# A decoder step on one core: the last gate tile copied raw, the gelus moved into the attention, the mixing behind them

## Chip, core and metric

The kernel runs on one core of one Trainium2 chip. The time is that of one execution on the device, in microseconds (us). Of several runs the median is given, and beside it the time of the one execution that was profiled.

## What is computed

One inference step of a hybrid decoder layer, for one new sequence of 512 tokens and eight sequences of four tokens each (544 tokens together), model width 1024, all in fp32. Cut to what matters here:

```
hn = _rmsnorm(x, g_pre_mix)
xl, gate, q, k, v, qi, ki, wi = _split_proj(hn @ w_in)
...
lru, hT, new_buf = _rglru(xl, conv_buf, h0, conv_w, conv_b, w_a, b_a, w_i, b_i, lam)
att = attend(q, k, v, qi, ki, wi)
mix = jnp.concatenate([lru * jax.nn.gelu(gate), att.reshape(B, T, ATTN_WIDTH)], axis=-1) @ w_out
x = x + _rmsnorm(mix, g_post_mix)
f = jnp.square(jax.nn.relu(_rmsnorm(x, g_pre_ffn) @ w_ff1)) @ w_ff2
x = x + _rmsnorm(f, g_post_ffn)
```

`_rglru` is a causal convolution of width 4, two sigmoid gates and a linear recurrence over the tokens, 512 channels. `attend` is sparse attention, 8 heads of width 64. For the 512 prompt tokens it goes over at most 512 keys, of which a mask keeps 128 for each token. For the 32 sample tokens it goes over 2048 cached keys and values in pages of 128, again under a mask. `lru * gelu(gate)` is the term whose pieces the change moves.

## The kernel before

The kernel is written by hand, engine by engine: each engine's program is a Python function that emits its instructions in a fixed order, and semaphores tie the engines together. Nothing is reordered by a scheduler. Everything is kept transposed, channels on the 128 partitions and the 544 tokens along the free dimension, in two halves of 272 (`HALF`).

**Products.** TensorE computes output tile after output tile into PSUM banks 0 to 3. Each half tile has a number; `gemm_mm` counts the finished ones, `gemm_ev` those that ScalarE has read out of PSUM. `E_GATE` is the first gate half, `E_WO` the first half of the output projection: when `gemm_ev` stands at `E_WO`, everything up to the last gate half is out of PSUM, and banks 0 to 3 are free for the attention.

**Gates.** The gate part has four tiles of 128 channels, in `mixT[:, 0:4, :]`. ScalarE copies the first three raw as they come (`gate_out`, L746 on). After the last step of the recurrence (`lru_root(3)`) it runs `gate_gelus`: gelu in place over tiles 0 to 2, then gelu straight from PSUM over the two halves of tile 3, which raises `gemm_ev` to `E_WO`. Square root, gelu and exponential each need a table load of their own on ScalarE.

**Attention over the prompt.** 32 units, `u = 8n + h`: query block n (0 to 3, with 128(n+1) keys) and head h. For each pair of units TensorE makes the scores (`att_scores`, banks 2 and 3), for each unit VectorE adds the mask and takes the maximum (`masked`), ScalarE the exponential with its sum (`exponentials`), VectorE divides (`normalized`), TensorE transposes (`att_transposes`, banks 6 and 7), ScalarE copies the transposes out (`transposed_out`), and for each pair TensorE multiplies with the values (`att_values`) and VectorE copies the result (`pair_out`). Each engine runs these steps in a loop over u, staggered: in turn u TensorE does the scores of u (even u), the transposes of u - 2 and the value pair u/2 - 2. The scores of a pair wait for both masks of the pair before (`pa_m`). Probabilities have four buffers, so `masked(u)` waits for the transposes of u - 4.

**Value products.** The sample attention's product with the cached values has 32 steps (`value_products(s)`, 4 matmuls in the program, 8 in the trace, about 1.0 us), into banks 4 and 5. Each needs four pages, 1 MB, in one of four slots. SyncE issues the transfers of step s as soon as product s - 4 has freed the slot (`values`, L399). Products 0 to 18 stand between the gate products, 19 to 31 in the attention: 19 in turn 0, then one in every third turn (20 in turn 1, 21 in turn 4, 22 in turn 7, 23 in turn 10, 24 in turn 13, and so on to 31 in turn 34). Slot 3 is in `regX`, the others are in `arena`.

**Others.** GpSimd waits for `gemm_ev` at `E_WO`, then loads the first half of the output weights (2 MB, L526). VectorE scales the first group of sample outputs (`sample_out(0)`) ahead of unit 0, and multiplies gate and recurrence (`mixed(c)`, L1172) in turns 8, 11, 14 and 17. The output projection waits for all units, all four mixings and the value pairs. Behind it come the MLP's products with split weights, about half of the run.

Of the kernel before, what the change touches and what calls it, by code (L numbers as in the profile page):

```python
# [16 lines left out]
ACT = mybir.ActivationFunctionType  # L17
# [8 lines left out]
HALF = NT // 2  # L26
# [5 lines left out]
CT = WIDTH // P  # L32
# [32 lines left out]
E_QI, E_KW, E_Q, E_K, E_V, E_XL, E_GATE, E_WO, E_MIX = 0, 8, 10, 18, 26, 31, 39, 47, 63  # L65
# [8 lines left out]
KSTEPS = GRP * NPG  # L74
# [2 lines left out]

V_ORDER = (4, 0, 1, 2, 3)
MID_VALUES = 19
NH_ORDER = (4, 5, 6, 7, 0, 1, 2, 3)  # L80
OUT_ORDER = ((0, 1, 2, 3, 4, 5, 6, 7), (4, 5, 6, 7, 0, 1, 2, 3))

# [7 lines left out]
def build(nc, xT_d, par_d, w_in_d, w_value_d, w_kw_d, w_out_d, w_mlp_d, wgate_d, ck_d, cv_d, ci_d, steps_d, pages_d,  # L90
          ident_d, rope_d, causal_d, ind_d, newmask_d, keyoff_d, yT_d, kT_d, v_d, kiT_d, lru_d):
    with ExitStack() as ctx:
# [87 lines left out]
        mixT = tiles(regM)  # L180
# [56 lines left out]
        half_cols = [slice(hf * HALF, (hf + 1) * HALF) for hf in range(2)]  # L237
# [305 lines left out]
        def _(eng):  # L543
# [7 lines left out]
            def gemm_out(e):  # L551
                eng.wait_ge(gemm_mm, e + 1)
                return bank[e % 4]
# [131 lines left out]
            def lru_root(c):  # L685
                eng.wait_ge(dd_rd, c + 1)
                nc.scalar.activation(dd, dd, ACT.Sqrt, scale=-1.0).then_inc(root_rd, 1)
# [60 lines left out]
                nc.scalar.copy(mixT[:, m, hf * HALF:(hf + 1) * HALF], src[:, 0:HALF]).then_inc(gemm_ev, 1)  # L748

            def gate_gelus():  # L750
                eng.wait_ge(gemm_ev, E_GATE + 6)
                for m in range(3):
                    nc.scalar.activation(mixT[:, m, :], mixT[:, m, :], ACT.Gelu_apprx_tanh).then_inc(gelu_rd, 1)
                for hf in range(2):
                    src = gemm_out(E_GATE + 6 + hf)
                    nc.scalar.activation(mixT[:, 3, half_cols[hf]], src[:, 0:HALF], ACT.Gelu_apprx_tanh).then_inc(gemm_ev, 1)

            sample_scores(30)
            sample_scores(31)
# [11 lines left out]
            def all_gates(c):  # L771
                for u in range(4):
                    lru_gates(c, u)
                lru_decay(c)
# [36 lines left out]
            lru_root(2)  # L811
            gate_out(2, 1)
            all_gates(3)
            lru_root(3)
            gate_gelus()

            def exponentials(u):
                nk = P * (u // NH + 1)
# [12 lines left out]
            for u in range(ATT_UNITS + 2):  # L831
                if u < ATT_UNITS:
                    exponentials(u)
                if u >= 2:
                    transposed_out(u - 2)
            load_tiles(eng, OUT1, range(CT))


# [105 lines left out]
        def _(eng):  # L944
# [221 lines left out]

            def mixed(c):

                eng.wait_ge(gelu_rd, min(c + 1, 3))
                eng.wait_ge(gemm_ev, E_WO)  # L1170
                eng.wait_ge(scan_rd, c + 1)
                vec.tensor_tensor(mixT[:, c, :], mixT[:, c, :], xl[:, c, 0:NT], ALU.mult).then_inc(mixed_rd, 1)  # L1172

# [57 lines left out]
            gated(3)  # L1231
            decayed(3)
            recurrent(3)
            sample_out(0)

            def masked(u):
                n, h = u // NH, u % NH
# [19 lines left out]
            for u in range(ATT_UNITS + 5):  # L1257
                if u < ATT_UNITS:
                    masked(u)
                if 1 <= u <= ATT_UNITS:  # L1260
                    normalized(u - 1)
                if u in (8, 11, 14, 17):
                    mixed((u - 8) // 3)
                if u >= 6 and u % 2 == 0:
                    pair_out((u - 6) // 2)

# [105 lines left out]
        def _(eng):  # L1372
# [388 lines left out]
            for u in range(ATT_UNITS + 5):  # L1761
                if u < ATT_UNITS and u % 2 == 0:
                    att_scores(u // 2)
                if 2 <= u < ATT_UNITS + 2:
                    att_transposes(u - 2)
                if 4 <= u < ATT_UNITS + 3 and u % 2 == 0:
                    att_values(u // 2 - 2)
                if u == 0:
                    value_products(MID_VALUES)
                elif u % 3 == 1 and MID_VALUES + 1 + u // 3 < KSTEPS:  # L1770
                    value_products(MID_VALUES + 1 + u // 3)

            def sample_out_transposes():
                for g in range(GRP):
# [185 lines left out]
```

## Time and profile before

| | us |
|---|---|
| median of 3 runs | 826.99 |
| lowest, highest | 825.69, 829.54 |
| the profiled execution | 830.0 |
| its span, first to last instruction | 828.2 |
| TensorE busy | 784.9 (95% of the span) |
| VectorE busy | 500.6 (60%) |
| ScalarE busy | 438.1 (53%) |
| mean granted TensorE clock | 0.983 of full |

The page divides the time by engine and by line; the chain that ended last says which work the end waited for. For a change of order, the timelines of single engines are the main view: each row has a start, a duration, and in square brackets the idle time ahead of it and what ended it. In the names, PE is TensorE, ACT ScalarE, DVE VectorE, POOL GpSimd, SPq the DMA issues of SyncE. `regX<-in_cv` is a transfer of cached values into slot 3.

### The profile page before, as it was taken

To read this page: it belongs to the slowest core of one execution; us is meant where nothing else is said; L and a number is where in the kernel's file an instruction comes from. 1 tells how busy PE (TensorE), PEld (TensorE's weight loads), DVE (VectorE), ACT (ScalarE), POOL (GpSimd) and SP (SyncE) were. 2 spreads that over 40 slices of the span, in tenths; PEclk is the share of its full clock that TensorE was granted. 3 is DMA by queue.
4 is the path that set the end of the run, shared out by engine and by line. 5 is a ranking of instruction groups with operands and counts; after the bars stand their busy time and mean duration, and the time that the engine had idled before them with its cause. 6 is when DMAs were issued, how large, how long until landed. Compare 5 with 4: busy or idle time off the path is not lost.

```text
span 828.2 us, 16951 instructions
## 1 busy us (share of the span) xinstructions
PE 784.9 (95%) x6187; PEld 655.8 (79%) x6187; DVE 500.6 (60%) x964; ACT 438.1 (53%) x881; POOL 101.5 (12%) x113
## 2 busy tenths in 40 slices
PE   5988999999999988999989999999999999999993
PEld 4862677745876643468879999999999999999993
DVE  4638999998664346621768786444446755544444
ACT  4546654412386574632457787534337777643440
POOL 0897453400000010000000000000000100000000
PEclk9998999999999998999999999999999999999997
DMA  8455339999649999460215555555555655555541
GB/s 325 138 169 159 122 134 370 384 393 362 223 134 353 326 340 355 147 248 17 76 55 175 178 175 169 173 172 175 177 177 178 214 173 176 177 178 176 170 161 54
DMA packets 69791, 166.89 MB, mean 202 GB/s; under 512 B 8995, under 2 KB 14628, under 8 KB 69348
## 3 DMA queue, kind: packets, MB, share of 16 engines
q1 hardware_dynamic: 64484, 145.54, 51.1%
q10 hardware_dynamic: 2592, 10.59, 3.6%
q0 software_dynamic: 2656, 9.98, 3.3%
q8 instruction: 36, 0.59, 0.3%
q14 instruction: 23, 0.19, 0.1%
HBM read 161.40 MB, written 4.67 MB: 201 GB/s over the span
## 4 chain that ended last, share of the span: by engine, by line
PE 78%; SPq 6%; ACT 5%; issue 4%; DVE 4%; DMA 2%; ACTq 0%; DVEq 0%
PE bank L1814 47%; PE bank L1393 14%; PE bank L1633 5%; SPq L399 5%; PE bank L1609 3%; PE bank L1731 1%; DMA regX<-in_cv 1%; PE bank L1503 1%; PE bank L1743 1%; SPq L394 1%; PE bank L1476 1%; DVE scp L1033 1%; PE bank L1756 1%; PE bank L1517 1%; DMA arena<-in_ck 1%
## 5 line engine op out<-in xcount | busy, mean ns | idle before, releaser
L1275 DVE TENSOR_TENSOR w_lo<-w_raw,w_hi 128x1024 fp32r<-128x1024 f32 x128 | 156.7, 1225 | 119.5 <-ACT w_hi L874 118.8
L874 ACT CAST w_hi<-w_raw 128x1024 fp32r<-128x1024 f32 x128 | 133.9, 1048 | 88.6 <-DMA w_raw<-in_w_mlp 88.6
L1814 PE MATMUL bank<-hn_hi,w_hi 128*128 128x272 f32 x512 | 148.6, 290 | 2.9 <-issue 2.9
L1814 PE MATMUL bank<-hn_hi,w_lo 128*128 128x272 f32 x512 | 148.8, 291 | 0.0
L1814 PE MATMUL bank<-h_lo,w_hi 128*128 128x272 f32 x512 | 148.4, 290 | 0.0
L1814 PE MATMUL bank<-hn_lo,w_hi 128*128 128x272 f32 x512 | 147.8, 289 | 0.0
L1814 PE MATMUL bank<-h_hi,w_hi 128*128 128x272 f32 x512 | 147.8, 289 | 0.0
L1814 PE MATMUL bank<-h_hi,w_lo 128*128 128x272 f32 x512 | 147.6, 288 | 0.0
L1814 PEld LDWEIGHTS bank<-hn_hi,w_hi 128*128 128x128 f32 x512 | 97.0, 190 | 3.4 <-issue 3.3
L1814 PEld LDWEIGHTS bank<-hn_lo,w_hi 128*128 128x128 f32 x512 | 97.1, 190 | 0.1
L1814 PEld LDWEIGHTS bank<-hn_hi,w_lo 128*128 128x128 f32 x512 | 96.9, 189 | 0.0
L1814 PEld LDWEIGHTS bank<-h_hi,w_hi 128*128 128x128 f32 x512 | 96.5, 188 | 0.0
L1814 PEld LDWEIGHTS bank<-h_hi,w_lo 128*128 128x128 f32 x512 | 96.4, 188 | 0.0
L1814 PEld LDWEIGHTS bank<-h_lo,w_hi 128*128 128x128 f32 x512 | 96.2, 188 | 0.0
L1393 PE MATMUL bank<-regM,wring 128*128 128x272 f32 x384 | 89.1, 393 | 0.0
L1393 PEld LDWEIGHTS bank<-regM,wring 128*128 128x128 f32 x384 | 72.8, 190 | 15.8 <-issue 0.8
L1393 PE MATMUL bank<-regR,wring 128*128 128x272 f32 x256 | 62.6, 398 | 0.0
L1393 PEld LDWEIGHTS bank<-regR,wring 128*128 128x128 f32 x256 | 47.5, 190 | 11.4 <-issue 2.4
L902 ACT ACTIVATE lx<-bank 128x272 f32<-128x272 f32 x64 | 25.5, 398 | 48.7 <-PE bank L1814 48.7
L1312 DVE TENSOR_TENSOR h_lo<-lx,h_hi 128x272 fp32r<-128x272 f32 x64 | 28.3, 442 | 34.6 <-ACT h_hi L908 33.7
L1287 DVE TENSOR_TENSOR regQ<-regQ 128x272 f32<-128x272 f32 x42 | 18.4, 440 | 47.6 <-ACT regM L916 19.2
L540 POOL DMA_DIRECT2D out<-regX x8 | 4.4, 544 | 289.0 <-DVE regX L1318 289.0
(260 smaller groups left out, 1209.8 us busy)
## 6 DMA issues: line engine op xcount, KB each, us to landing
w_raw<-in_w_mlp SPq DMA_DIRECT2D x128, 512.0 KB, 3.4
arena<-in_ck SPq DMA_DIRECT2D x96, 256.0 KB, 4.4
arena<-in_cv SPq DMA_DIRECT2D x96, 256.0 KB, 4.2
regQ<-in_ck SPq DMA_DIRECT2D x32, 256.0 KB, 4.5
regX<-in_cv SPq DMA_DIRECT2D x32, 256.0 KB, 3.9
wring<-in_w_in ACTq DMA_DIRECT2D x12, 512.0 KB, 5.9
wring<-in_w_in SPq DMA_DIRECT2D x8, 512.0 KB, 8.8
regX<-in_xT SPq DMA_DIRECT2D x4, 544.0 KB, 6.0
```

Source lines behind the costliest of these rows:

```text
L394: eng.load(page_regs, steps[0:1, bass.ds(s * 4, 4)])
L399: eng.dma_start(slot[:, b4, :], table[bass.ds(page[b4], 1), :, :].rearrange("a p c -> p (a c)")).then_inc(landed, 16)
L874: nc.scalar.copy(w_hi[n % 4][:, :], w_raw[n % 4][:, :]).then_inc(w_hi_rd, 1)
L902: nc.scalar.activation(relu_t[:, t % 2, :], bank[q % 4][:, 0:HALF], ACT.Relu).then_inc(mlp_ev, 1)
L1033: ins = vec.scalar_tensor_tensor(out=acc, in0=sm[:, u % 2, 0:nk], scalar=w, in1=acc, op0=ALU.mult, op1=ALU.add)
L1275: vec.tensor_tensor(w_lo[n % 4][:, :], w_raw[n % 4][:, :], w_hi[n % 4][:, :].bitcast(F32), ALU.subtract).then_inc(w_lo_rd, 1)
L1287: ins = vec.tensor_tensor(sqT[:, total, c], sqT[:, total, c], sqT[:, order[k], c], ALU.add)
L1312: vec.tensor_tensor(h_lo[:, at], square_t[:, t % 2, :], h_hi[:, at].bitcast(F32), ALU.subtract).then_inc(h_lo_rd, 1)
L1393: ins = pe.matmul(bank[e % 4][0:parts, 0:HALF], lhs(k), rhs[:, k, hf * HALF:(hf + 1) * HALF], start=(k == 0), stop=(k == KT - 1))
L1609: ins = pe.matmul(bank[4 + g][32 * b4:32 * b4 + 32, :], pT_rows[g][:, r, 32 * b4:32 * b4 + 32], v_slot[s % SLOTS][:, b4, :], start=(r == 0 ...
L1633: ins = pe.matmul(bank[e % 4][:, 0:HALF], lhs, rhs, start=(first and n == 0 and name == passes[0]), stop=(last and n == KT - 1 and name == ...
L1814: ins = pe.matmul(out, lhs[s][:, k * P:(k + 1) * P], rhs(k), start=(first and k == 0 and i == 0), stop=(last and k == KT - 1 and i == 2))
```

## The change

`gate_out` now copies tile 3 raw too, its first half ahead of `lru_root(3)`, its second behind it; the second copy raises `gemm_ev` to `E_WO`. `gate_gelus` becomes one group of four gelus over whole tiles, in ScalarE's turn 15 of the attention, behind `transposed_out(13)`. Value products 24, 25 and 26 go from turns 13, 16 and 19 to turn 17, all three in a row. `mixed` goes from turns 8, 11, 14, 17 to turns 21, 23, 25, 27, and `sample_out(0)` from ahead of unit 0 into turn 2. Line numbers grow by two or three.

```diff
+GELU_UNIT = 15
+VALUE_UNITS = (0, 1, 4, 7, 10, 17, 17, 17, 22, 25, 28, 31, 34)
...
             def gate_gelus():
-                eng.wait_ge(gemm_ev, E_GATE + 6)
-                for m in range(3):
+                eng.wait_ge(gemm_ev, E_WO)
+                for m in range(CT):
                     nc.scalar.activation(mixT[:, m, :], mixT[:, m, :], ACT.Gelu_apprx_tanh).then_inc(gelu_rd, 1)
-                for hf in range(2):
-                    src = gemm_out(E_GATE + 6 + hf)
-                    nc.scalar.activation(mixT[:, 3, half_cols[hf]], src[:, 0:HALF], ACT.Gelu_apprx_tanh).then_inc(gemm_ev, 1)
...
             all_gates(3)
+            gate_out(3, 0)
             lru_root(3)
-            gate_gelus()
+            gate_out(3, 1)
...
                 if u >= 2:
                     transposed_out(u - 2)
+                if u == GELU_UNIT:
+                    gate_gelus()
...
-                eng.wait_ge(gelu_rd, min(c + 1, 3))
-                eng.wait_ge(gemm_ev, E_WO)
+                eng.wait_ge(gelu_rd, c + 1)
...
             recurrent(3)
-            sample_out(0)
...
-                if u in (8, 11, 14, 17):
-                    mixed((u - 8) // 3)
+                if u == 2:
+                    sample_out(0)
+                if u in (21, 23, 25, 27):
+                    mixed((u - 21) // 2)
...
-                if u == 0:
-                    value_products(MID_VALUES)
-                elif u % 3 == 1 and MID_VALUES + 1 + u // 3 < KSTEPS:
-                    value_products(MID_VALUES + 1 + u // 3)
+                for i, at_unit in enumerate(VALUE_UNITS):
+                    if at_unit == u:
+                        value_products(MID_VALUES + i)
```

The order of instructions at the three places where it matters follows. First ScalarE from the end of the last recurrence step to the first exponentials, before (L753 and L756 are the gelus, L687 the root, L820 the exponentials):

```order
L683 ACTIVATE lx<-lx,sp 128x544
L687 ACT_TABLE_LOAD
L687 ACTIVATE lx<-lx 128x544 [waits dd_rd]
L753 ACT_TABLE_LOAD
L753 ACTIVATE regM<-regM 128x544 [waits gemm_ev]
L753 ACTIVATE regM<-regM 128x544 x2
L756 ACTIVATE regM<-bank1 128x272 [waits gemm_mm]
L756 ACTIVATE regM<-bank2 128x272 [waits gemm_mm]
L820 ACT_TABLE_LOAD
L820 ACTIVATE arena,stat<-arena,stat 128x128 [waits pa_m] x2
```

And the same place in the changed kernel (L750 is the raw copy, L689 the root):

```order
L750 COPY regM<-bank1 128x272 [waits gemm_mm]
L689 ACT_TABLE_LOAD
L689 ACTIVATE lx<-lx 128x544 [waits dd_rd]
L750 COPY regM<-bank2 128x272 [waits gemm_mm]
L820 ACT_TABLE_LOAD
L820 ACTIVATE arena,stat<-arena,stat 128x128 [waits pa_m] x2
```

One table load and five gelus have gone from ahead of the exponentials; two copies stand on either side of the root. The second place is ScalarE around the attention's turn 15 in the changed kernel (L755 the gelus, L820 exponentials of units 15, 16 and 17, L829 copies of units 13, 14 and 15; before, the rows of L755 and the second load are not there):

```order
L820 ACTIVATE regR,stat<-regR,stat 128x256 [waits pa_m]
L829 COPY arena<-bank7 128x256 [waits pa_t]
L755 ACT_TABLE_LOAD
L755 ACTIVATE regM<-regM 128x544 [waits gemm_ev]
L755 ACTIVATE regM<-regM 128x544 x3
L820 ACT_TABLE_LOAD
L820 ACTIVATE arena,stat<-arena,stat 128x384 [waits pa_m]
L829 COPY regR<-bank6 128x256 [waits pa_t]
L820 ACTIVATE arena,stat<-arena,stat 128x384 [waits pa_m]
L829 COPY regR<-bank7 128x256 [waits pa_t]
```

Two table loads now stand between two exponentials. The third place is TensorE from the scores of unit 16 to those of unit 18, before (L1731 scores, L1743 transposes, L1756 value pairs, L1609 value products):

```order
L1731 MATMUL bank<-arena,regQ 128x384 [waits pa_m]
...
L1743 MATMUL bank<-ident,regR 128x128 [waits pa_te,pa_n]
...
L1756 MATMUL bank<-arena 64x128 [waits pa_oe,pa_te]
...
L1609 MATMUL bank<-arena 32x512 [waits v_in1]
L1609 MATMUL bank<-arena 32x512 x3
L1743 MATMUL bank<-ident,regR 128x128 [waits pa_te,pa_n]
...
L1731 MATMUL bank<-arena,regQ 128x384 [waits pa_m]
```

And after (L1733 scores, L1745 transposes, L1758 value pairs, L1611 value products):

```order
L1733 MATMUL bank<-arena,regQ 128x384 [waits pa_m]
...
L1745 MATMUL bank<-ident,regR 128x128 [waits pa_te,pa_n]
...
L1758 MATMUL bank<-arena 64x128 [waits pa_oe,pa_te]
...
L1745 MATMUL bank<-ident,regR 128x128 [waits pa_te,pa_n]
...
L1611 MATMUL bank<-arena 32x512 [waits v_in0]
...
L1611 MATMUL bank<-arena 32x512 [waits v_in1]
...
L1611 MATMUL bank<-arena 32x512 [waits v_in2]
...
L1733 MATMUL bank<-arena,regQ 128x384 [waits pa_m]
```

Before, product 25 alone stands ahead of the transposes of unit 15; after, products 24, 25 and 26 stand behind them.

## Rows read from the trace of the kernel before

**Rows 1.** The page's chain that ended last: share of the span by engine.
```profile
PE 78%; SPq 6%; ACT 5%; issue 4%; DVE 4%; DMA 2%; ACTq 0%; DVEq 0%
```

**Rows 2.** Timeline of ScalarE at the handover: start, duration, instruction, idle before.
```profile
299.66 1.28 ACT L753 ACT_TABLE_LOAD   x1
300.95 1.75 ACT L753 ACTIVATE regM<-regM 128x544 f32<-128x544 f32 x3
302.61 0.66 ACT L756 ACTIVATE regM<-bank 128x272 f32<-128x272 f32 x2
303.29 1.28 ACT L820 ACT_TABLE_LOAD   x1
304.58 0.40 ACT L820 ACTIVATE arena<-arena,stat 128x128 f32<-128x128 f32 x1
```

**Rows 3.** Timeline of TensorE, units 0 to 20.
```profile
300.59 1.06 PE L1609 MATMUL bank<-arena 128*32 128x512 f32 x8
303.32 0.49 PE L1731 MATMUL bank<-arena,regQ 64*128 64x128 f32 x4 [1.67 <-ACT regM L756]
...
316.54 1.93 PE L1609 MATMUL bank<-regX,arena 128*32 128x512 f32 x8 [0.32 <-DMA regX<-in_cv]
...
319.02 1.23 PE L1731 MATMUL bank<-arena,regQ 64*128 64x256 f32 x4
...
322.47 1.24 PE L1609 MATMUL bank<-arena 128*32 128x512 f32 x8
323.64 0.70 PE L1731 MATMUL bank<-arena,regQ 64*128 64x256 f32 x4
...
326.50 0.92 PE L1731 MATMUL bank<-arena,regQ 64*128 64x384 f32 x4 [0.73 <-DVE stat L1243]
...
333.23 0.92 PE L1731 MATMUL bank<-arena,regQ 64*128 64x384 f32 x4
```

**Rows 4.** Timelines of VectorE and of GpSimd's DMA issues.
```profile
302.09 0.75 DVE L1193 TENSOR_SCALAR regR<-bank,sstat 128x512 f32<-128x512 f32 x1
...
313.44 0.72 DVE L1172 TENSOR_TENSOR regM<-regM,arena 128x544 f32<-128x544 f32 x1
...
336.95 0.56 DVE L1243 CUSTOM_DVE_ANT_0 regR<-bank,scp 128x384 f32<-128x384 f32 x1 [0.47 <-PE bank L1731]
...
303.56 2.10 POOL L526 DMA_DIRECT2D wring<-in_w_out  x4 [23.21 <-ACT regM L756]
```

**Rows 5.** The chain that ended last, in order of time, 300 to 330 us.
```profile
306.90 9.60 DMA regX<-in_cv
...
325.18 0.72 DVE regM L1172
```

**Rows 6.** Timeline of SyncE's DMA issues, value steps 21 to 23.
```profile
300.18 3.55 SPq L399 DMA_DIRECT2D arena<-in_cv  x6
305.03 2.29 SPq L399 DMA_DIRECT2D regX<-in_cv  x4
```

**Rows 7.** DMA issues of 304 to 308 us: count, KB each, median us to landing.
```profile
regX<-in_cv SPq DMA_DIRECT2D x4, 256.0 KB, 8.8
```

**Rows 8.** Busy time by stretch: us, five engines, granted clock, DMA share, GB/s.
```profile
302.00:304.00 2.00, 0.68 (x8) 0.46 (x12) 0.96 (x4) 1.98 (x5) 0.44 (x1) 1.00 0.98 313
...
314.00:316.00 2.00, 1.24 (x10) 0.70 (x10) 1.64 (x9) 0.79 (x4) 0.00 (x0) 1.00 1.04 395
316.00:318.00 2.00, 1.68 (x12) 0.20 (x8) 1.93 (x7) 1.42 (x5) 0.00 (x0) 0.51 1.06 388
...
322.00:324.00 2.00, 2.00 (x14) 0.64 (x14) 0.18 (x1) 0.72 (x3) 0.00 (x0) 0.78 1.06 388
```

**Rows 9.** Timeline of ScalarE around turns 15 to 17.
```profile
326.98 0.35 ACT L829 COPY arena<-bank 128x256 f32<-128x256 f32 x1
328.04 0.61 ACT L820 ACTIVATE arena<-arena,stat 128x384 f32<-128x384 f32 x1 [0.71 <-DVE stat L1243]
...
329.79 0.35 ACT L829 COPY regR<-bank 128x256 f32<-128x256 f32 x1
```

## The prediction

> **What bounds the kernel now.** I read the chain that ended last first. Four fifths of it are TensorE [rows 1], so the change moves the end of the kernel only by what it moves of the start of the output projection, which follows the 32 attention units without a gap. Nothing behind that is edited. So the question is what paces TensorE from 300 to 361 us.
>
> I then read ScalarE, TensorE and VectorE in order of time, from the last gate product on. **Stretch 1, the handover (300.6 to 303.3).** TensorE ends its last gate work and value product 18 at 301.65 and idles 1.67 us until ScalarE has released `E_WO` [rows 3]. ScalarE spends that time on a table load and five gelus, and loads the table for the exponentials behind them: the first exponential starts at 304.58 [rows 2]. **Stretch 2, units 0 to 10.** Units are short here, and the three engines wait for each other. It ends at 316.54 with a wait of 0.32 us for the DMA of value step 23, whose four transfers were issued from 305.03 on [rows 3, 6]. The chain has 9.60 us of that DMA in it [rows 5]. Transfers issued then take a median of 8.8 us [rows 7], since all DMA engines are full (share 0.98 to 1.06, [rows 8]) and carry the output weights as well. **Stretch 3, units 10 to 16.** TensorE's granted clock falls to its lower level (1.2 GHz) at about 316.0, after 2 us with 1.24 us of work, and is back at 2.4 GHz at about 322.9 (0.78 is the mean of that slice, [rows 8]). **Stretch 4, units 16 on.** TensorE is nearly full: the scores of unit 16 start at 326.50, those of unit 20 at 333.23 [rows 3], and they set the pace.
>
> **The change part by part.** Times below are on the profile's clock (before: span 828.2, execution 830.0).
>
> *Part A, raw copy instead of gelus before unit 0.* The copies of tile 3 go one on either side of `lru_root(3)`. The product's last matmul leaves TensorE at 300.6, so the second copy (0.39 as the two halves in [rows 2] take 0.38 each) ends at about 301.1, where `E_WO` fell at 303.3 before. TensorE is then at value product 18 until 301.65, so unit 0 starts with no wait: **-1.67 us**. The exponential table load follows the copy directly, 301.1 to 302.4, hidden behind VectorE's scan (to 302.0) and the first scores. No more than 1.67 can be won here.
>
> *Part B, `sample_out(0)` from before unit 0 to behind unit 2.* Its main instruction takes 0.75 us and ended at 302.84 [rows 4], before the first scores were even started (303.32, [rows 3]): free before. A reciprocal belongs to it, some 0.9 us in all from the end of the scan on. In unit 2 it stands ahead of `masked(3)`, and the scores of the next pair wait for that mask. The two engines wait for each other in turn there, so little of it is hidden: I take **+0.8** (0.4 to 0.9).
>
> *Part C, mixing 0 out of unit 8.* 0.72 us, 0.64 to the next instruction, ahead of `masked(9)`, for which TensorE waits [rows 4]: **-0.64**. So TensorE arrives at value product 23 at 316.22 - 1.67 + 0.8 - 0.64 = 314.7.
>
> *Part D, the DMA of step 23.* The same bytes have to land ahead of it. The output weights, issued by GpSimd at 303.56 on `E_WO` [rows 4], are now issued at 301.3. From 302 to 304 the DMA moved 313 GB/s, from 316 on 388 [rows 8]. Filling 2.3 us at the higher rate is 2.3 x 75 = 0.17 MB, at 388 GB/s 0.45 us earlier. Its own issue can come only 1.0 us earlier: SyncE is busy with the transfers of step 22 until 303.7 [rows 6], and the slot that it takes is free at 303.0. So it lands between 315.5 and 316.5; I take 316.0, as the queue was full, **-0.5**. The 1.5 us won above shrink to 0.5: TensorE waits 1.3 us instead of 0.32.
>
> *Part E, units 10 to 16 without value products 24 and 25.* Product 24 goes, 322.47 to 323.64: **-1.17**. The scores of unit 14 move up into the time at the low clock: 1.23 instead of 0.70 there, **+0.5**. Mixing 2 stood on the chain at 325.18 [rows 5] ahead of `masked(15)`: **-0.64**. Unit 16's scores start at 326.50 - 0.5 - 1.17 + 0.5 - 0.64 = 324.7. Mixing 1 fell into a VectorE wait, and counts for nothing.
>
> *Part F, the gelu group behind `transposed_out(13)`.* It is one load to gelu, four gelus, one load back: 1.28 + 4 x 0.553 (300.95 to 302.61 for three, [rows 2]) + 1.28 = 4.78 us. The copy of unit 13 ended at 327.33 [rows 9], now at 325.5; exponential 16 starts at 325.5 + 4.78 = 330.3 instead of 328.04. Queued behind the group on ScalarE are exponential 16, copy 14, exponential 17 and copy 15; VectorE's normalizations wait for the first, TensorE's transposes 16 and value pair 7 for the others. Meanwhile TensorE does the scores of unit 16, transposes 14, value pair 6, transposes 15 (to 326.9), then value products 24 to 26 (3 x 1.0, to 329.9), then the scores of unit 18 (to 330.8). Then it is out of work: transposes 16 wait for exponential and normalization (331.5), value pair 7 for copy 15. From exponential 16 to the end of copy 15 before were 2.1 us [rows 9], so copy 15 ends at 332.4; value pair 7 (0.6), transposes 17 (0.5) bring the scores of unit 20 to 333.5. Before they started at 333.23 [rows 3], product 26 included. So from unit 10 to 20 all that parts D and E won is given back: **+0.3 against before at unit 20**.
>
> The Trainium skill speaks against this part ("ScalarE: Activation LUTs", Table sets: the hidden batching unit): group calls by table set, and it counts a switch at about 2.7 us with the drain. The trace has 1.28 from the start of a load to the next instruction, twice [rows 2], with no drain. By the page's figure the group would be 2.8 us longer and the sum +3.3 at unit 20; the sum goes by the rows.
>
> *Part G, mixing in units 21, 23, 25, 27.* Each (0.72) stands just ahead of an even unit's mask, where VectorE waits for scores; the shortest such wait is 0.47 [rows 4], the others are longer. Cost 0.17 where it is short: **+0.2**. Without that cover it would be 4 x 0.64 = 2.6. Value loads 28 to 30 wait for the slots of products 24 to 26, free at 328 to 330; each is due at unit 25 or later (after 341): no wait.
>
> **Sum:** +0.3 + 0.2 = +0.5 on 830.0, so 830.5 for an execution like the profiled one. That execution is 3.0 above the median of the runs (826.99), so **827.5 us** on the scale of the runs. A measurement of this kernel can tell about 0.5%, 4.1 us, from no change.
>
> **The rivals.**
> *1. TensorE's clock doesn't fall at 316, or for less time (faster).* For: after 302 to 304, with 0.68 busy of 2 us, it did not fall, and that hole is now closed [rows 8]. Against: the wait ahead of product 23 gets longer, 1.3 us. 6.8 us at half clock cost up to 3.4 us; part E's +0.5 would go too, but VectorE and ScalarE then take part of it. I give it -3: 824.5.
> *2. A second fall after the gelu group (slower).* One mechanism: transposes 16 and value pair 7 wait for the four ScalarE steps behind the group. TensorE idles about 0.7 + 0.4 us from 330.8 to 332.4, about as much as just before the fall at 316 (0.76 of 2 us idle, [rows 8]). What follows is dense TensorE work, so 6.8 us at the low clock cost the full 3.4: 831. [...] Against: 3 us of unbroken value products stand ahead of it.
> *3. Output weights crowd step 22.* Issued 2.3 us earlier, they share the engines with load 22, issued 301.3 to 303.7. At step 23's latency (8.8, [rows 7]) it lands at 312. Product 22, which started at 310.97 and would be due 0.87 us earlier, waits 1.9 us, and product 23 comes at about 316.6 instead of 316.0: +0.6, 828.1. The Trainium skill ("DMA: Bandwidth & Descriptors", Queues, rings and completion order) has each DMA engine take turns between the queues that it has work for. By that rule, this rival holds; the 8.8 us beside the weights agree.
> *4. The landing follows the issue, and the group costs less.* Step 23 lands at 315.5 and TensorE meets copy 15 with no hole: -1.5, 825.5.
>
> **How the numbers follow.** My forecast with its small terms 0.50, rival 1 0.14, rival 2 0.16, rival 3 0.10, rival 4 0.10. All within 0.5%, except the far ends of rivals 1 and 2 together with the others' terms: faster by over 0.5% (under 822.9) 0.06, slower (over 831.1) 0.09, same 0.85. The range takes in rival 1 with a lighter end and rival 2: 823.8 to 831.2.
>
> **What would show it.** Right: no idle time before unit 0's scores; a wait of 1 to 2 us for `regX<-in_cv` before product 23; one gelu load and one exponential load 3.5 us apart at 325 to 330; a hole of about 1 us on TensorE behind the scores of unit 18; the output projection within 1 us of 361.3. Wrong: a second stretch at the low clock between 330 and 361, product 23 over 1 us earlier than 316.5, or a wait of the scores for VectorE in units 22 to 28.

## The result, and the profile after

The changed kernel takes 833.12 us (median of 16 executions, 830.97 to 836.13), the kernel before 828.13 beside it (16, 825.69 to 835.94). The ratio is 1.0057, interval 1.0040 to 1.0073: **slower by 4.7 us** by the ratio, by more than the 0.5% that the prediction set as its bound, and outside its range (823.8 to 831.2). The execution profiled took 834.25, its span 832.4, the mean granted clock 0.982.

Where the time went is best read on TensorE, measured from the start of value product 18 (the last one ahead of the attention) to the first matmul of the output projection, since the two profiled executions differ by 1.1 us already ahead of it. Timeline of TensorE of the changed kernel: start, duration, instruction, idle time before it and what ended that. They answer [rows 3] (L1611 are value products, L1733 scores, L1745 transposes, L1395 the output projection).

```profile
301.69 1.06 PE L1611 MATMUL bank<-arena 128*32 128x512 f32 x8
302.69 0.49 PE L1733 MATMUL bank<-arena,regQ 64*128 64x128 f32 x4
...
307.30 0.49 PE L1733 MATMUL bank<-arena,regQ 64*128 64x128 f32 x4 [0.74 <-DVE stat L1243]
...
314.76 1.93 PE L1611 MATMUL bank<-arena 128*32 128x512 f32 x8 [3.56 <-DMA arena<-in_cv]
...
321.70 1.94 PE L1611 MATMUL bank<-regX,arena 128*32 128x512 f32 x8
...
328.61 0.92 PE L1733 MATMUL bank<-arena,regQ 64*128 64x384 f32 x4
...
331.01 2.78 PE L1611 MATMUL bank<-arena 128*32 128x512 f32 x24
333.72 0.92 PE L1733 MATMUL bank<-arena,regQ 64*128 64x384 f32 x4
335.78 0.55 PE L1745 MATMUL bank<-ident,arena 128*128 128x128 f32 x3 [1.15 <-DVE arena L1250]
...
337.45 0.92 PE L1733 MATMUL bank<-arena,regQ 64*128 64x384 f32 x4
...
365.52 3.93 PE L1395 MATMUL bank<-regM,wring 128*128 128x272 f32 x16
```

The output projection of the kernel before, in the same view (the rows ahead of it are [rows 3]):

```profile
361.31 0.95 PE L1393 MATMUL bank<-regM,wring 128*128 128x272 f32 x3
```

| us after the start of value product 18 | before | after | difference |
|---|---|---|---|
| scores of unit 0 | 2.73 | 1.00 | -1.7 |
| value product 22, when TensorE is ready for it | 10.38 | 9.51 | -0.9 |
| value product 22 starts | 10.38 | 13.07 | +2.7 |
| value product 23 starts | 15.95 | 20.01 | +4.1 |
| scores of unit 16 | 25.91 | 26.92 | +1.0 |
| scores of unit 20 | 32.64 | 35.76 | +3.1 |
| output projection | 60.72 | 63.83 | +3.1 |

The handover works (no idle time before unit 0), then product 22 waits 3.56 us for its cached values. Before, it did not wait at all. The chain that ended last in the changed kernel has that transfer in it, and the weights' issue on GpSimd comes just ahead of it:

```profile
304.85 9.87 DMA arena<-in_cv
```
```profile
302.48 2.11 POOL L528 DMA_DIRECT2D wring<-in_w_out  x4 [21.02 <-ACT regM L750]
```

In [rows 4] the weights were issued at 303.56, that is 2.97 us behind the start of product 18; now it is 0.79 us. Step 22's four transfers were issued from 301.3 to 303.7 before, ahead of the weights; now from 302.9 to 304.85, beside and behind the four transfers of the weights. The DMA issues of the two stretches, count, KB each and median us to landing, first before (301.3 to 304), then after (302.9 to 304.9):

```profile
arena<-in_cv SPq DMA_DIRECT2D x4, 256.0 KB, 4.3
```
```profile
wring<-in_w_out POOLq DMA_DIRECT2D x4, 512.0 KB, 8.2
arena<-in_cv SPq DMA_DIRECT2D x4, 256.0 KB, 8.9
```

The latency doubled. And the clock, the second part of the loss, falls inside the wait. Busy time by stretch of the changed kernel (the five engines, granted clock, DMA share, GB/s), which answers [rows 8]:

```profile
310.00:312.00 2.00, 1.05 (x8) 0.48 (x6) 1.43 (x9) 1.29 (x6) 0.00 (x0) 1.00 1.03 410
312.00:314.00 2.00, 0.00 (x0) 0.00 (x0) 0.00 (x0) 0.00 (x0) 0.00 (x0) 0.96 1.03 398
314.00:316.00 2.00, 1.24 (x8) 0.20 (x8) 0.00 (x0) 0.00 (x0) 0.00 (x0) 0.50 1.05 394
...
322.00:324.00 2.00, 2.00 (x10) 0.29 (x2) 0.42 (x2) 0.60 (x2) 0.00 (x0) 0.50 1.08 384
324.00:326.00 2.00, 1.98 (x17) 1.07 (x16) 1.07 (x6) 1.01 (x4) 0.00 (x0) 0.98 0.80 248
```

TensorE has nothing to do from 311.2 to 314.76; at about 313.8 its clock falls to 1.2 GHz (0.96 is the mean of the slice to 314), and it comes back to 2.4 at about 324. So 9.3 us of work run at the low level, where it was 6.4 before (316.54 to about 322.9).

### The profile page after: what moved, and what is told of

Its sections match the earlier page's. It is cut to its first block, busy times and chain, and to the rows that moved or that the text cites. A ratio compares the mean times of both kernels' runs of the same rounds, so it can differ in the third digit from the quotient of the medians.

```text
span 832.4 us, 16953 instructions
## 1 busy us (share of the span) xinstructions
PE 786.7 (95%) x6187; PEld 656.7 (79%) x6187; DVE 499.9 (60%) x964; ACT 440.4 (53%) x883; POOL 100.8 (12%) x113
## 4 chain that ended last, share of the span: by engine, by line
PE 81%; ACT 4%; DVE 4%; DMA 4%; issue 4%; SPq 3%; ACTq 0%; DVEq 0%
PE bank L1815 47%; PE bank L1395 15%; PE bank L1635 5%; PE bank L1611 3%; SPq L401 2%; PE bank L1505 2%; PE bank L1733 1%; DMA regQ<-in_ck 1%; DMA arena<-in_cv 1%; DVE scp L1035 1%; PE bank L1519 1%; PE bank L1745 1%; PE bank L1478 1%; PE bank L1758 1%; DMA arena<-in_ck 1%
## 5 line engine op out<-in xcount | busy, mean ns | idle before, releaser
L1395 PE MATMUL bank<-regM,wring 128*128 128x272 f32 x384 | 89.6, 394 | 0.0
L1395 PEld LDWEIGHTS bank<-regM,wring 128*128 128x128 f32 x384 | 73.4, 191 | 16.0 <-issue 0.8
L1395 PE MATMUL bank<-regR,wring 128*128 128x272 f32 x256 | 62.6, 398 | 0.0
L1395 PEld LDWEIGHTS bank<-regR,wring 128*128 128x128 f32 x256 | 47.5, 190 | 11.4 <-issue 2.4
```

The costliest lines, as they stand in the source:

```text
L1395: ins = pe.matmul(bank[e % 4][0:parts, 0:HALF], lhs(k), rhs[:, k, hf * HALF:(hf + 1) * HALF], start=(k == 0), stop=(k == KT - 1))
```

## The experiments

**Theories.** *Weights:* the earlier release of `E_WO` lets GpSimd issue the 2 MB of output weights ahead of step 22's transfers; product 22 waits, the clock falls, and this is the whole loss. *Group:* the gelus and the displaced mixing and value products in units 15 to 20 cost more than parts A to E win. *Sample:* `sample_out(0)` in turn 2, with its wait of 0.74 us, is what starts it. Times of the kernel before are from the same chip in the same rounds.

All twelve, with the stretch from value product 18 to the output projection in the profiled execution, and the wait of TensorE for cached values:

| kernel | median, us | before beside it | ratio and interval | stretch, us | wait, us |
|---|---|---|---|---|---|
| before, weights late | 826.28 | 827.73 | 0.9988 (0.9976 to 1.0001) | 57.62 | 0 |
| after, weights late | 827.63 | 827.73 | 0.9991 (0.9974 to 1.0008) | 56.71 | 0 |
| before, weights early | 832.49 | 827.73 | 1.0056 (1.0034 to 1.0077) | 63.72 | 3.09 |
| after, values back | 836.43 | 827.73 | 1.0105 (1.0083 to 1.0127) | 65.61 | 3.08 |
| after, weights behind step 22 | 830.97 | 828.04 | 1.0036 (1.0018 to 1.0053) | 58.38 | 0 |
| after, weights late, values back | 830.54 | 828.04 | 1.0033 (1.0015 to 1.0051) | 59.82 | 0 |
| after, weights late, group at the end | 828.21 | 828.04 | 0.9997 (0.9982 to 1.0013) | 57.09 | 0 |
| after, weights late, sample first | 823.81 | 828.04 | 0.9957 (0.9940 to 0.9973) | 55.90 | 0 |
| after, sample first | 831.95 | 827.61 | 1.0057 (1.0035 to 1.0079) | 61.75 | 4.40 |
| before, sample in turn 2 | 828.58 | 827.61 | 1.0009 (0.9992 to 1.0025) | 61.44 | 0 |
| four products | 829.59 | 827.61 | 1.0014 (0.9997 to 1.0031) | 61.11 | 3.50 |
| four products, weights last | 823.54 | 828.02 | 0.9946 (0.9933 to 0.9959) | 55.19 | 0 |

### The weights, late and early

The first edit holds GpSimd's load of the output weights back until value product 23 is counted (`v_mm` 24), in the changed kernel and in the one before:

```diff
             eng.wait_ge(gemm_ev, E_WO)
+            eng.wait_ge(v_mm, 24)
             for m in range(CT):
                 eng.dma_start(wring[:, 0, m * PIECE:(m + 1) * PIECE], w_out_d[m]).then_inc(out_in[m], 16)
```

> The changed kernel, with one wait more on GpSimd: the output weights are issued only when value product 23 is done (24 steps), not on E_WO. Theory 1 (the weights, issued ahead of the transfers of value step 22, make product 22 wait 3.6 us and bring the low clock on early and for longer): the wait before product 22 goes, the low clock lasts at most 7 us, and the time falls by about 3 us against the changed kernel, to about that of the kernel before (ratio to before 0.998 to 1.002). Theory 2 (the gelu group with its two table loads inside the attention is what costs): the wait before product 22 may go, but the gain is under 1 us and the ratio stays at 1.004 or more.

> The kernel before, with the same wait on GpSimd: output weights issued behind value product 23. Theory 1: the DMA of step 23 lands 3 to 4 us earlier, TensorE no longer waits before product 23, the low clock from 316 on shrinks or goes, and the kernel is 1 to 3 us faster than before (ratio 0.996 to 0.999). Theory 2: no difference (ratio 1.000 within 0.001).

The second does to the kernel before what the change does to this load alone: it goes when the last gate half is computed and not when it is out of PSUM, with all else as it was.

```diff
-            eng.wait_ge(gemm_ev, E_WO)
+            eng.wait_ge(gemm_mm, E_WO)
```

> The kernel before, with the output weights issued when the last gate product has left TensorE (gemm_mm) instead of when ScalarE has read it (gemm_ev): about 2.5 us earlier, and nothing else changed. Theory 1: this alone costs 1 to 3 us (ratio 1.001 to 1.004), seen as a wait before value product 22 or 23 for its transfers. Theory 2: no cost, ratio 1.000 within 0.001.

Measured: with the weights late the changed kernel takes 827.63, and the loss is gone. The kernel before with late weights isn't clearly faster than as it was (0.9988, interval to 1.0001). With the weights early the kernel before takes 832.49, a ratio of 1.0056, as large as that of the whole change (1.0057) and more than the 1 to 3 us that were expected. Timelines of TensorE, then GpSimd, and the chain, of the kernel before with early weights:

```profile
316.18 1.93 PE L1609 MATMUL bank<-arena 128*32 128x512 f32 x8 [3.09 <-DMA arena<-in_cv]
```
```profile
303.01 2.10 POOL L526 DMA_DIRECT2D wring<-in_w_out  x4 [20.61 <-PE bank L1633]
```
```profile
306.22 9.92 DMA arena<-in_cv
```

It is the same wait at the same product for the same transfer, with no gelu, mixing or value product moved. Its clock falls twice for 3.4 us each (at about 315.7 and 322.6) where that of the changed kernel falls once for 10.2; the path to the projection is as long (63.72 and 63.83). Of the changed kernel with late weights, TensorE from product 18 over product 22 (310.04, no wait), units 16 and 20 to the output projection, GpSimd, and two of the stretches:

```profile
300.58 1.07 PE L1612 MATMUL bank<-arena 128*32 128x512 f32 x8
...
310.04 1.07 PE L1612 MATMUL bank<-arena 128*32 128x512 f32 x8
...
314.56 1.06 PE L1612 MATMUL bank<-regX,arena 128*32 128x512 f32 x8
...
320.37 0.92 PE L1734 MATMUL bank<-arena,regQ 64*128 64x384 f32 x4
...
329.21 0.92 PE L1734 MATMUL bank<-arena,regQ 64*128 64x384 f32 x4
...
357.29 3.93 PE L1396 MATMUL bank<-regM,wring 128*128 128x272 f32 x16
```
```profile
316.26 2.10 POOL L529 DMA_DIRECT2D wring<-in_w_out  x4 [35.91 <-PE bank L1612]
```
```profile
312.00:314.00 2.00, 1.50 (x11) 0.74 (x11) 1.60 (x10) 1.50 (x6) 0.00 (x0) 1.00 1.02 278
314.00:316.00 2.00, 2.00 (x18) 0.65 (x17) 1.75 (x9) 1.46 (x5) 0.00 (x0) 1.00 1.04 394
```

The four transfers of its step 22, with no weights issued yet (DMA issues of 301.7 to 304.5):

```profile
arena<-in_cv SPq DMA_DIRECT2D x4, 256.0 KB, 3.9
```

Product 23 has no wait either, the clock stays at its upper level through the attention, and the stretch is 56.71 us. What follows: the *weights* theory is right, and it is the whole loss.

The pair of late kernels also tells what the other parts of the change are worth with this disturbance out of the way. The kernel before with late weights, from product 18 over unit 16 to the projection:

```profile
299.33 1.06 PE L1610 MATMUL bank<-arena 128*32 128x512 f32 x8
...
322.15 0.92 PE L1732 MATMUL bank<-arena,regQ 64*128 64x384 f32 x4 [0.74 <-DVE stat L1244]
...
356.95 3.93 PE L1394 MATMUL bank<-regM,wring 128*128 128x272 f32 x16
```

The stretch is 56.71 against 57.62, **0.9 us less** on the path. The medians don't show it (827.63 and 826.28). The profiled execution of the changed one (824.47) is the fastest of its twelve. By the executions' mean clocks the rest may be the clock: all 12 of the kernel before with late weights have 0.987 or more, of the changed one 7 of 12 have 0.986 or less. What its clock fell at in those is in no profile.

### The value products back in their turns

```diff
-VALUE_UNITS = (0, 1, 4, 7, 10, 17, 17, 17, 22, 25, 28, 31, 34)
+VALUE_UNITS = (0, 1, 4, 7, 10, 13, 16, 19, 22, 25, 28, 31, 34)
```

> The changed kernel with value products 24, 25 and 26 back in turns 13, 16 and 19; the gelu group stays in turn 15 without cover. Theory 1: the wait before product 22 stays as it is; the group's hole on TensorE grows from 1.2 to about 3 us, of which part is won back where the products stood, so 1 to 2 us slower than the changed kernel (ratio to before 1.007 to 1.009). Theory 2 (the group is the cost): 3 us slower than the changed kernel (ratio 1.009 or more).

> Output weights late (behind product 23), gelu group in turn 15, value products 24 to 26 back in turns 13, 16 and 19. It shows the group's own cost where the DMA is out of the way. My theory: the hole behind unit 18's scores grows from 1.1 to about 3 us, and the three products cover the rest of it where they are moved: 1.5 to 2.5 us slower than with the three products in turn 17 (ratio to before 1.001 to 1.003), or up to 4 us slower if the clock falls behind the hole. Rival (placing products beside the group is worth nothing): same as with them in turn 17, ratio 0.998 to 1.000.

Measured: 3.3 us more than the changed kernel with the weights early (836.43 against 833.12, not on the same chip; ratios 1.0105 and 1.0057), and 2.9 us more with them late (830.54 against 827.63, again on two chips, ratios 1.0033 and 0.9991). The first of these, taken alone, is what was expected if the *group* theory held (1.009 or more). But the second kernel has the same group uncovered and no loss from the weights, and it stands at 1.0033: most of the 1.0105 isn't the group's. Behind the scores of unit 18, TensorE of the second (weights late) and the two stretches of 4 us around it, the timeline row first:

```profile
330.47 0.55 PE L1746 MATMUL bank<-ident,arena 128*128 128x128 f32 x3 [3.09 <-DVE arena L1251]
```
```profile
328.00:332.00 4.00, 1.53 (x14) 1.04 (x14) 2.13 (x8) 3.95 (x10) 0.00 (x0) 1.00 1.05 399
332.00:336.00 4.00, 4.00 (x18) 1.22 (x19) 1.21 (x7) 1.09 (x4) 0.00 (x0) 0.57 0.76 266
```

The hole is 3.09 us, where the three value products left 1.15, and the clock falls behind it (0.57 is a mean over four microseconds). So the moved products do what they are there for: they cover about 2 us of the group, and behind them the clock stayed up. The fall that rival 2 describes is here, behind a hole of 3.1 us; behind the hole of 1.15 there was none in the profiled execution of the changed kernel.

### The group behind the attention

```diff
-GELU_UNIT = 15
-VALUE_UNITS = (0, 1, 4, 7, 10, 17, 17, 17, 22, 25, 28, 31, 34)
+GELU_UNIT = ATT_UNITS + 1
+VALUE_UNITS = (0, 1, 4, 7, 10, 13, 16, 19, 22, 25, 28, 31, 34)
...
-                if u in (21, 23, 25, 27):
-                    mixed((u - 21) // 2)
...
+            for c in range(CT):
+                mixed(c)
```

> Output weights late, the gelu group and the four mixings behind the last attention unit, value products in their old turns. My theory: no hole in the middle and no table load back to the exponentials; instead the output projection waits 2 to 3 us for the group and the mixings at its end. Sum against the weights-late kernel between -1 and +1.5 us: ratio to before 0.998 to 1.001. Rival (the group costs its full 4.8 us wherever it stands): ratio 1.003 or more.

Measured: 828.21, no difference from before. In the attention nothing is lost, but the output projection waits for the gelus and mixings, and the clock falls there, at about 358.7. Its first row (the view names no engine for the wait; the four mixings, L1174, run from 356.12 to 358.75):

```profile
358.86 5.51 PE L1397 MATMUL bank<-regM,wring 128*128 128x272 f32 x16 [1.60 <-issue]
```

Its stretches there, with the same columns as the ones above:

```profile
356.00:360.00 4.00, 2.40 (x15) 1.09 (x12) 3.46 (x6) 1.73 (x4) 1.83 (x3) 0.84 0.88 306
360.00:364.00 4.00, 4.00 (x15) 3.12 (x14) 0.00 (x0) 0.00 (x0) 0.00 (x0) 0.74 1.09 450
```

The 16 matmuls take 5.51 us against 3.93 in the others. So a group at unit 15 is no worse than one that ends the attention (0.9991 and 0.9997). The place of the group isn't the loss, and that speaks against the *group* theory.

### Weights behind step 22 only

```diff
             eng.wait_ge(gemm_ev, E_WO)
+            eng.wait_ge(v_mm, 20)
```

> The changed kernel with the output weights held back until value product 19 is done (20 steps), at about 304 us: only 1.5 us later than in the changed kernel, but behind the last transfers of value step 22. Theory 1a (what counts is the place in the queues: whatever is issued behind the weights is late): product 22 waits for less than 1 us, product 23 takes the delay as in the kernel before, ratio to before 0.999 to 1.002. Theory 1b (2 MB more in the same stretch cost the same wherever they come in before product 23): product 22 or 23 waits 3 us or more, ratio 1.004 or more.

Measured: 830.97, spread 825.85 to 833.41, between the changed kernel and that with late weights. Of the two expectations neither is met: product 22 has no wait, as the first says, but the ratio is 1.0036. The profiled execution was the fastest one, a stretch of 58.38 with a short fall of the clock at product 21, so it doesn't show where the others lose their time. Its chain and its DMA issues (302.5 to 305) do show which step now stands beside the weights, issued at 301.88:

```profile
304.72 9.64 DMA regX<-in_cv
```
```profile
regX<-in_cv SPq DMA_DIRECT2D x4, 256.0 KB, 8.9
```

Step 23's data lands at 314.36 and its product starts at 314.41. TensorE comes no earlier only because of the fall at product 21: with the clock up it would be ready 13.98 us behind product 18, as in the kernel with late weights, at 312.7. My estimate from these rows is thus a wait of 1.6 us in such an execution. That the others lose their time there is not shown; that the threshold has to lie further back is.

### `sample_out(0)` first again, and in turn 2 of the kernel before

```diff
             recurrent(3)
+            sample_out(0)
...
-                if u == 2:
-                    sample_out(0)
```

> Output weights late, everything else as in the changed kernel, but the first sample output scaled ahead of unit 0 again. My theory: the wait of unit 4's scores for VectorE (0.74 us) goes, and the kernel gains 0 to 0.8 us against the one with the weights late (ratio to before 0.997 to 0.999), less if the exponential table load hides nothing of it. Rival: it delays the first mask by 0.9 us and the gain of the early handover is lost (ratio 1.000).

> The changed kernel with one edit undone: the first sample output is scaled ahead of unit 0 again; the output weights stay early. Theory 1 (the early weights are the cause, the move of the sample output costs its 0.8 us and little more): product 22 still waits 3 us or more, and the kernel is at most 1 us faster than the changed one (ratio to before 1.004 to 1.006). Theory 3 (the sample output in turn 2 is worth about 3 us wherever it stands, since it tips the clock): ratio 1.001 to 1.003.

> The kernel before with only the first sample output moved into turn 2. Theory 1: +0.8 us in the attention, of which the wait for the transfers of step 23 takes some back, ratio 1.000 to 1.001. Theory 3: more executions show the clock's fall, ratio 1.002 to 1.004.

Measured: the stretch gets 0.81 us shorter with the weights late (55.90 against 56.71), which is part B by its forecast of 0.8, and the kernel takes 823.81, **faster than before by 3.6 us** by the ratio. The median moved by 3.8 us between the two (2.8 by the ratios, as they ran on different chips), not by 0.8: its clocks are 0.989 or more in five executions of six, and those of the kernel that it is compared with only in two of twelve. With the weights early, sample first doesn't help: 831.95, ratio 1.0057 again, since product 22 is then due still earlier, and waits longer for its data:

```profile
313.13 1.94 PE L1610 MATMUL bank<-arena 128*32 128x512 f32 x8 [4.40 <-DMA arena<-in_cv]
```

Put into turn 2 of the kernel before, it makes no difference that the measurement can tell (828.58, 1.0009). A mean clock of 0.985 or less is in 5 of its 12 executions and in 5 of 23 beside it, too few to tell. The *sample* theory falls as the cause; it is a price of 0.8 us beside it.

### A fourth product under the group, and the best kernel

```diff
-VALUE_UNITS = (0, 1, 4, 7, 10, 17, 17, 17, 22, 25, 28, 31, 34)
+VALUE_UNITS = (0, 1, 4, 7, 10, 17, 17, 17, 17, 25, 28, 31, 34)
```

with sample first and weights behind product 23; the second kernel has this, and the weights behind product 28 (`v_mm` 29).

> Output weights late, first sample output ahead of unit 0, and value product 27 moved from turn 22 to turn 17 as well, so that four products stand beside the gelu group. The hole of 1.1 us behind unit 18's scores should be filled and about 1.0 us be won where product 27 stood: 1 us faster than with three products (823.8), ratio to before 0.993 to 0.996. Rival: the scores of unit 18 come 1.0 us later and the masks behind them hold up unit 20, so nothing is won (ratio as with three, 0.9957).

> As the kernel with four products beside the gelu group, but the output weights held back until value product 28 is done (29 steps, about 337 us), so that they stand behind the transfers of step 27 instead of beside them. Theory 1 (whatever value step is in transfer beside the weights comes 4 to 5 us late, and it costs when its product is due then): the 3.5 us wait before product 27 goes, no value product waits for a transfer, no fall of the clock in the attention, 823 us or less, ratio to before 0.993 to 0.996. Rival (four products in a row hold up the masks, and that is what cost): ratio 0.999 or more.

Measured: the first takes 829.59 (1.0014), worse than with three products (823.81), which neither expectation had. The weights, issued at 314.79, now stand ahead of step 27's transfers, and product 27 is due early:

```profile
327.58 1.94 PE L1611 MATMUL bank<-regX,arena 128*32 128x512 f32 x8 [3.50 <-DMA regX<-in_cv]
```
```profile
317.17 10.37 DMA regX<-in_cv
```

It is the loss of the changed kernel again, at another step, and the rival (the scores of unit 18 hold up the rest) isn't it, as the next kernel shows. With the weights last, the same product has its data, the hole under the group is down to 0.28 us, and the kernel is the best of all at **823.54, 0.9946 of before** (interval 0.9933 to 0.9959):

```profile
323.90 1.04 PE L1611 MATMUL bank<-regX,arena 128*32 128x512 f32 x8
...
326.07 0.55 PE L1745 MATMUL bank<-ident,arena 128*128 128x128 f32 x3 [0.28 <-DVE arena L1252]
...
355.12 3.93 PE L1395 MATMUL bank<-regM,wring 128*128 128x272 f32 x16
```

Its weights go at 337.97, 17 us ahead of the projection, and the projection has no wait. Against the kernel with three products (823.81, in another round) it can't be told apart.

## Why the prediction was wrong

*Parts A and B were right.* Unit 0's scores wait for nothing (1.67 forecast and won). Unit 4 waits 0.74 for the mask, and TensorE is ready for product 22 0.87 us earlier: -1.67 + 0.8. The runs with sample first put part B at 0.81.

*Part C was right where the data was there, and part E only by its sum.* Between the two kernels with late weights, from product 18, product 23 comes 1.56 us earlier (13.98 against 15.54). Product 22 is 0.92 earlier there (9.46 against 10.38), which leaves 0.64, part C's forecast. Unit 16 comes 3.0 us earlier (19.79 against 22.82): 1.47 for part E, forecast 1.31. But the 1.31 holds +0.5 for work at the low clock, and neither of these two kernels has a low clock there: without it the forecast would be 1.81, so that part of the agreement is luck.

*Part F was right.* From the scores of unit 16 to those of unit 20 the changed kernel takes 8.84 us where it was 6.73: +2.1; forecast 8.8. The group, from its load to exponential 16, on ScalarE of the changed kernel, which answers [rows 9]:

```profile
329.46 1.28 ACT L755 ACT_TABLE_LOAD   x1
330.76 2.30 ACT L755 ACTIVATE regM<-regM 128x544 f32<-128x544 f32 x4
333.07 1.28 ACT L820 ACT_TABLE_LOAD   x1
334.37 0.61 ACT L820 ACTIVATE arena<-arena,stat 128x384 f32<-128x384 f32 x1
```

4.91 us against 4.78. The sum went by the rows and not by the larger price of a table switch that the prediction quoted from the Trainium skill ("ScalarE: Activation LUTs", Table sets: the hidden batching unit), and the trace bears the rows out: 1.30 from the start of a load to the next instruction, both times. The hole behind unit 18's scores is 1.15 (forecast about 1.1 in two pieces). *Part G* was near: the difference stays at 3.1 from unit 20 to the projection, where +0.2 was forecast.

*Part D failed, and the loss on the path is in it.* It put product 23 at 316.0, 0.5 us earlier than before; it came at 320.6 on the clock of before (321.70 less the 1.1), 4.1 later. It asked whether the data of step 23 lands in time, and took for granted that step 22, whose wait was zero before, kept its data. Rival 3 asked that question and had the right mechanism; it mis-sized it. By it product 22 waits 1.9 us (landing at 312), product 23 comes at 316.6, the price is +0.6. Measured: a wait of 3.56, product 23 at 320.6 on the same clock. Two terms were wrong:
- *The landing.* I took step 23's 8.8 us from about 303.2, so 312. The last of step 22's transfers was issued at 304.85 and took 9.87: 314.7, or 313.6 on the clock of before. So it lands 1.6 later, 0.5 for the later issue (303.7 and not 303.2, and the last of the four is what counts) and 1.1 for the latency. The weights themselves went when part D said: 302.48 is 301.4 on the clock of before, forecast 301.3.
- *The clock.* Rival 3 costed the wait as shifted by idle time only, and let the fall stand at 316, as in [rows 8]. But the fall came ahead of the end of the longer wait (at about 313.8, 312.7 on the clock of before), and 9.3 us of work run at the low level instead of 6.4.

From -0.9 at product 22 these make +2.7 at its start and +4.1 at product 23. From there to unit 16 the changed kernel gives back 3.1, more than part E's 1.3, since only 2.3 us of its low clock are left behind the start of product 23, of 6.4 before; part F takes 2.1: +3.1.

*The size of the miss has two halves.* Forecast 827.5, measured 833.1. On the path +3.1 came for +0.5; that alone would have made 830.1, still inside the range. The other 3.0 us are the credit for the median, to which the next paragraph comes. That the halves add up to the measured 5.6 is in part chance: the two profiled executions differ by 1.1 us ahead of product 18 as well. Two slips of the prediction's sums change nothing in this: rival 4's -1.5 makes 826.0 and not 825.5, and with a group longer by 2.8 us, +3.3 is the whole sum and not the state at unit 20 (+3.1). Of its signs of being wrong none came (no low clock after 330, no product 23 over 1 us early, no long wait in units 22 to 28): none of them watched product 22. Of its signs of being right the wait before product 23 and the projection within 1 us of 361.3 (364.4 on the clock of before) failed.

*The profile I argued from was not the usual one.* Of the 86 executions of the kernel before that ran beside the experiments, 63 have a mean clock of 0.987 or more (median 827.45), 22 one of 0.985 or less (median 829.92). The one profiled, 830.0 at 0.983, is among the latter, while all 16 of the changed kernel have 0.979 to 0.983. What their clocks suggest, without a profile of one that shows it: in the usual execution of before, the clock doesn't fall ahead of product 23, just as it doesn't in the kernel before with late weights (57.62 us where the profiled one took 60.72). Against that, the loss is larger than the two profiles show, up to 63.83 - 57.62 = 6.2 us on the stretch; the ratio says 4.7 of the whole. To take 3.0 us off "for the median" was therefore to give the changed kernel a credit for high clocks that none of its 16 executions has. (Of the 16 executions of before the median is 828.13, so even for that kernel the credit would have been 1.9.) Rival 1 could have been read as a warning: it asked whether the fall of 316 is fixed, but only for the changed kernel.

*Rivals 1, 2 and 4 did not occur.* The low clock lasted longer, not shorter. Behind the hole under the group (1.15 us) there was no second fall; in the kernels without value products there (3.1 us) it came. The landing didn't follow the issue, and the group cost what part F said.

## What to carry over

When a change releases something earlier, list every engine that waits on that semaphore: here GpSimd's prefetch of 2 MB, due 60 us later, moved ahead of a streamed load of 1 MB that was due 9 us later, and one wait for it undid all the gains. Issue a bulk prefetch by its own need, behind the last streamed load whose step has no slack, and not by the first moment at which its buffer is free. And before arguing from a profiled execution, place its time and mean clock among the other runs: a clock fall seen in it may be absent from most.

## What was not expected of the hardware

- Transfers of 256 KB landed in a median of 3.9 us with no weights issued, of 4.3 when the weights were behind them, and of 8.9 with the weights beside and ahead; those that the chains show took 9.87, 9.92, 9.64 and 10.37 us in four kernels. The DMA engines were as good as full in the second case too (share 0.98 from 302 to 304, [rows 8]): a full share doesn't say whether a transfer waits 4 or 10 us, what else is queued does. That fits the rule of taking turns between queues which the prediction cites from the Trainium skill ("DMA: Bandwidth & Descriptors", Queues, rings and completion order).
- The clock fell within idle times of TensorE of 3.1 to 4.4 us, or up to 1.8 us behind them, in each profiled kernel with such a hole in the attention, with one exception: in the changed kernel with its values back it was low from 310.0 on, 3 us ahead of the hole before product 22. It never fell behind the hole of 1.15. After shorter idle times it is not the same from one execution to the next. At the handover TensorE's program is the same in the kernel before and in the one with sample in turn 2, and so is its idle time (1.67), but in [rows 8] the clock stays up from 302 to 304, and in the other it falls:

```profile
302.00:304.00 2.00, 1.62 (x12) 0.69 (x16) 0.51 (x4) 1.97 (x5) 1.37 (x3) 0.72 1.05 363
304.00:306.00 2.00, 2.00 (x12) 0.21 (x4) 0.57 (x2) 0.52 (x4) 1.79 (x10) 0.50 0.97 330
```

Ahead of the MLP, TensorE idles 2.85 us in all of them; in the profile of before its clock falls behind that (at about 425.2), in the changed kernel with late weights it doesn't. What decides stays open: the profiles don't show it, and no run was made for it.
